# Score products of prompt attention in pairs of units, their low parts on half the array each

## The reference

```python
z = jnp.einsum('bqhd,bkhd->bhqk', q, k) * (HEAD_DIM ** -0.5)
z = z + sb_bias[None, :, None, None]
mask = kpos[None, :] < qpos[:, None]
l = jnp.where(mask, jax.nn.log_sigmoid(-z), 0.0)
later = jnp.flip(jnp.cumsum(jnp.flip(l, -1), -1), -1) - l
w = jnp.where(mask, jnp.exp(jax.nn.log_sigmoid(z) + later), 0.0)
out = jnp.einsum('bhqk,bkhd->bqhd', w, v)
```

## Time and profile before

| | |
|---|---|
| median of three timed runs | 2445.37 us (2442.97 to 2445.67) |
| span of the profiled execution | 2440.8 us (its own total time is not on the page) |
| busy: PE, its weight loads, DVE, ACT | 99%, 96%, 65%, 53% |
| score products on the low part of the keys | 160, from 410 to 1578 us |

### The profile page before, as it was taken

One profiled execution on the slowest core, in us unless ns is written; L12 is line 12 of the kernel. 1 busy time (PEld: TensorE's weight loads), 2 busy tenths in 40 slices (PEclk: granted clock), 3 DMA queues, 4 the chain that ended last, 5 costly groups with the idle time before them and its releaser, 6 DMA issues.

```text
span 2440.8 us, 36724 instructions
## 1 busy us (share of the span) xinstructions
PE 2406.7 (99%) x13263; PEld 2331.5 (96%) x13263; DVE 1585.0 (65%) x2233; ACT 1286.6 (53%) x1982; POOL 243.0 (10%) x527
## 2 busy tenths in 40 slices
PE   7999999999999999999999999999999999999998
PEld 7999999999999999999999999999999999999998
DVE  7635662656777787777788777757655665764335
ACT  5466523555655745656555565554455555444432
POOL 0012320200001100011100111000122130000000
PEclk9999999999999999999999999999999999999999
DMA  8434554534444434444443443333566674343332
GB/s 257 153 108 143 159 174 138 184 111 130 162 134 139 142 110 144 150 129 144 128 124 117 137 141 124 125 122 114 182 187 187 209 234 134 120 136 117 112 118 83
DMA packets 141526, 351.64 MB, mean 144 GB/s; under 512 B 20625, under 2 KB 64146, under 8 KB 141218
## 3 DMA queue, kind: packets, MB, share of 16 engines
q1 hardware_dynamic: 128994, 312.88, 40.6%
q0 software_dynamic: 12352, 36.42, 4.7%
HBM read 300.11 MB, written 49.12 MB: 143 GB/s over the span
## 4 chain that ended last, share of the span: by engine, by line
PE 95%; DVE 2%; ACT 2%; DMA 1%; issue 1%; SPq 0%; DVEq 0%; ACTq 0%
PE PS L1136 22%; PE PS L1138 22%; PE PS L1137 22%; PE PS L874 5%; PE PS L872 5%; PE PS L873 5%; PE PS L942 2%; PE PS L964 1%; PE PS L932 1%; PE PS L963 1%; PE PS L1026 1%; PE PS L933 1%; PE PS L1056 1%; PE PS L1014 1%; PE PS L912 1%
## 5 line engine op out<-in xcount | busy, mean ns | idle before, releaser
L1440 ACT ACTIVATE w_hi_lo<-w_raw 128x1024 fp32r<-128x1024 f32 x240 | 252.7, 1053 | 283.5 <-PE PS L1138 277.3
L1136 PE MATMUL PS<-a_hi,w_hi_lo 128*128 128x416 f32 x1080 | 385.1, 357 | 1.3 <-DVE w_hi_lo L1995 1.3
L1138 PE MATMUL PS<-a_hi,w_hi_lo 128*128 128x416 f32 x1080 | 379.3, 351 | 0.0
L1137 PE MATMUL PS<-a_lo,w_hi_lo 128*128 128x416 f32 x1080 | 378.6, 351 | 0.0
L1995 DVE TENSOR_TENSOR w_hi_lo<-w_raw,w_hi_lo 128x1024 fp32r<-128x1024 f32 x240 | 292.6, 1219 | 58.1 <-ACT w_hi_lo L1440 55.9
L1136 PE MATMUL PS<-h_hi,w_hi_lo 128*128 128x416 f32 x824 | 294.6, 358 | 0.0
L1138 PE MATMUL PS<-h_hi,w_hi_lo 128*128 128x416 f32 x824 | 290.2, 352 | 0.0
L1137 PE MATMUL PS<-h_lo,w_hi_lo 128*128 128x416 f32 x824 | 289.4, 351 | 0.0
L2022 DVE TENSOR_TENSOR h_lo<-h_full,h_hi 128x416 fp32r<-128x416 f32 x160 | 94.6, 592 | 222.9 <-ACT h_hi L1455 222.8
L1136 PEld LDWEIGHTS PS<-a_hi,w_hi_lo 128*128 128x128 f32 x1080 | 203.0, 188 | 4.1 <-DVE w_hi_lo L1995 1.7
L1137 PEld LDWEIGHTS PS<-a_lo,w_hi_lo 128*128 128x128 f32 x1080 | 203.5, 188 | 2.1
(11 more groups left out here) (336 smaller groups left out, 5203.8 us busy)
## 6 DMA issues: line engine op xcount, KB each, us to landing
w_raw<-w_all SPq DMA_DIRECT2D x380, 512.0 KB, 3.5
proj_scratch<-stage SPq DMA_DIRECT2D x70, 208.0 KB, 1.9
k_rows<-kv_out SPq DMA_DIRECT2D x80, 128.0 KB, 4.0
v_hi_lo<-v_scratch SPq DMA_DIRECT2D x40, 256.0 KB, 4.1
x_scratch<-x_full SPq DMA_DIRECT2D x20, 416.0 KB, 2.9
x_residual<-x_scratch SPq DMA_DIRECT2D x5, 1664.0 KB, 7.6
pages<-ck SPq DMA_DIRECT2D x64, 128.0 KB, 2.2
pages<-ck POOLq DMA_DIRECT2D x64, 128.0 KB, 2.5
```

Of the source, the lines that this page charges most:

```text
L1136: pe.matmul(out, w_h, mh_[:, k, :], start=(g == 0), stop=False)
L1137: pe.matmul(out, w_h, ml_[:, k, :], start=False, stop=False)
L1138: ins = pe.matmul(out, w_l, mh_[:, k, :], start=False, stop=(g == KT - 1))
L1440: act.activation(halves(w_hi(n)), raw_halves(n), ACT.Copy).then_inc(s_wh, 1)
```

## The change

Units are scored in pairs in the even slots. The two products with the keys' high part stay as they are. The product with the low part now takes the high part of q alone: 64 rows, rows 0 to 63 for the even unit and 64 to 127 for the odd one. For that, DVE puts the low part of q into the lower rows of odd units and the upper rows of even units (the product of the two low parts is left out). Even units use bank 6, odd ones bank 4. Bank 4 is thus no longer free for the value tiles: they are turned in bank 3, between the last sum of one head and the first of the next. Such a turn waits for the head before (`HEADS_BEFORE`), and the first sum of a head waits for the tiles turned so far. Steps and slots of the turns are moved accordingly.

```diff
-V_AT_STEP = {78: 0, 81: 1, 83: 2}
-V_AT_SLOT = {24: 3, 40: 4, 60: 5, 80: 6, 110: 7}
+V_AT_STEP = {78: 0, 82: 1, 84: 2}
+V_AT_SLOT = {28: 3, 44: 4, 64: 5, 88: 6, 116: 7}
+HEADS_BEFORE = (0, 1, 2, 5, 7, 9, 11, 13)
...
-    return len(V_AT_STEP) + len([t for t in V_AT_SLOT if t < tau])
+    return len([j for j in V_AT_STEP if 2 * (j - 78) < tau]) + len([t for t in V_AT_SLOT if t < tau])
+
+
+def z_bank(t):
+
+    return 4 if t % 2 else 6
...
-            def scores(t):
-
-                v, i, w, top = unit(t)
+            def scores_two(t):
+
+                v, i, _, _ = unit(t)
...
-                q = qs[:, (c * NH + h) % 2, i * P:(i + 1) * P]
-                pe.matmul(PS[:, 6, 0:w], q, khl[:, v % 2, 0, 0:w], start=True, stop=False)
-                pe.matmul(PS[:, 6, 0:w], q, khl[:, v % 2, 1, 0:w], start=False, stop=True).then_inc(s_z, 1)
+                for d in range(2):
+                    w = unit(t + d)[2]
+                    q = qs[:, (c * NH + h) % 2, (i + d) * P:(i + d + 1) * P]
+                    pe.matmul(PS[:, z_bank(t + d), 0:w], q, khl[:, v % 2, 0, 0:w], start=True, stop=False)
+                for d in range(2):
+                    w = unit(t + d)[2]
+                    high = slice(HD * d, HD * d + HD)
+                    q = qs[high, (c * NH + h) % 2, (i + d) * P:(i + d + 1) * P]
+                    pe.matmul(PS[:, z_bank(t + d), 0:w], q, khl[high, v % 2, 1, 0:w], start=False, stop=True).then_inc(s_z, 1)
...
                 if m:
-                    pe.wait_ge(s_vlo, m)
+                    pe.wait_ge(s_yc, HEADS_BEFORE[m])
                 for j in range(4):
-                    ins = pe.transpose(PS[:, 4, j * P:(j + 1) * P], vmk[:, 0, j, :].bitcast(F32), ident[:, :])
+                    ins = pe.transpose(PS[:, 3, j * P:(j + 1) * P], vmk[:, 0, j, :].bitcast(F32), ident[:, :])
...
+                if v in FIRST:
+                    pe.wait_ge(s_vlo, v_tiles_done(4 * v + 6))
...
-                if tau < N_UNITS:
-                    scores(tau)
+                if tau < N_UNITS and tau % 2 == 0:
+                    scores_two(tau)
...
-                dve.tensor_tensor(qs[HD:P, w % 2, :], qst[HD:P, :], qs[HD:P, w % 2, :].bitcast(F32), ALU.subtract).then_inc(s_qlo, 1)
+                full = qst[:, :].rearrange("p (i two q) -> p two i q", two=2, q=P)
+                parts_ = qs[:, w % 2, :].rearrange("p (i two q) -> p two i q", two=2, q=P)
+                for odd, low in ((0, slice(HD, P)), (1, slice(0, HD))):
+                    ins = dve.tensor_tensor(parts_[low, odd], full[low, odd], parts_[low, odd].bitcast(F32), ALU.subtract)
+                ins.then_inc(s_qlo, 1)
```

More of the change, by code:

```diff
@@ L1383, in round_v @@
                 act.wait_ge(s_vtr, m + 1)
-                act.activation(vmk[:, :, :, 0:HD], PS[:, 4, :].rearrange("p (j h d) -> p h j d", h=2, d=HD), ACT.Copy).then_inc(s_vhi, 1)
+                act.activation(vmk[:, :, :, 0:HD], PS[:, 3, :].rearrange("p (j h d) -> p h j d", h=2, d=HD), ACT.Copy).then_inc(s_vhi, 1)
             def sigmoids(t):
@@ L1394, in sigmoids @@
                     act.wait_ge(s_tr, t - 2)
-                act.activation(sP[:, t % 3, 0:w], PS[:, 6, 0:w], ACT.Sigmoid, scale=HD ** -0.5, bias=bias_h[:, h:h + 1])
+                act.activation(sP[:, t % 3, 0:w], PS[:, z_bank(t), 0:w], ACT.Sigmoid, scale=HD ** -0.5, bias=bias_h[:, h:h + 1])
                 if t >= 5:
@@ L1398, in sigmoids @@
                     act.wait_ge(s_car, t)
-                act.activation(nP[:, t % 5, 0:w], PS[:, 6, 0:w], ACT.Sigmoid, scale=-HD ** -0.5, bias=nbias_h[:, h:h + 1]).then_inc(s_sn, 1)
+                act.activation(nP[:, t % 5, 0:w], PS[:, z_bank(t), 0:w], ACT.Sigmoid, scale=-HD ** -0.5, bias=nbias_h[:, h:h + 1]).then_inc(s_sn, 1)
             def round_w(t):
@@ L1939, in round_v @@
                 dve.wait_ge(s_vhi, m + 1)
-                dve.tensor_tensor(vmk[:, :, :, HD:P], PS[:, 4, :].rearrange("p (j h d) -> p h j d", h=2, d=HD),
+                dve.tensor_tensor(vmk[:, :, :, HD:P], PS[:, 3, :].rearrange("p (j h d) -> p h j d", h=2, d=HD),
                                   vmk[:, :, :, 0:HD].bitcast(F32), ALU.subtract).then_inc(s_vlo, 1)
```

## The result

The changed kernel takes 2455.18 us (median of four runs, 2454.19 to 2455.59), the kernel before 2444.17 (four runs, 2441.43 to 2445.67): 1.0046 of it, with an interval of 1.0033 to 1.006. It is slower by 11.0 us. The forecast was slower by 22.4: the direction and the place are right, and the size is twice what was measured. The time lies in the forecast's range, but only because that was taken down through the unchanged case; it is under the likeliest case's own range (2457 to 2477). All times here are of runs at a granted clock of 0.996 to 0.998; one run among the experiments, at 0.557, took 4016 us and is left out.

What follows compares the result with a forecast made beforehand. The prediction took the matrix engine, busy 99% of the span, as the bound. Low products in pairs +24.4 us and the wait that goes -2 gave +22.4; 2445.4 + 22.4 = 2468 us, slower by 0.9%, range 2441 to 2480.

Steps and rivals of the forecast that it cites:

- the unchanged case: Low products do not overlap and no way in and out is paid: 2443 us, no change; chance 0.09, with mixed cases.
- the likeliest case: Low products pay for a change of mode, 80 times: slower, own range 2457 to 2477 us, chance 0.74.
- What bounds the kernel: Whole span: matrix engine busy 99%, 95% of the last chain; only its work or gaps gain or lose time.
- The way in: Before a pair's first low product: 0.09 us of emptying, then 0.11 for a 128-column load, 0.20 in all.
- Between the two low products: Within a pair's low part: the second product starts 0.11 us after the first, and they overlap from there.
- rival 2: The mode changes, but a pair's low products start together: +15.6 - 2, 2459 us; counted in the 0.74 for slower.
- The way out: Behind a pair's low products: 0.08 us of emptying and 0.11 until the next product streams, 0.19 in all.
- The wait that goes: Three odd units' score products no longer wait for the sigmoid emptying bank 6: between nothing and 2.7 us, taken as -2.
- Value tiles and the q split: Value tiles turned in bank 3, and the vector engine's q subtraction split into two halves: cost 0 each.
- 1 (no mode, 2430): 64 rows are no other mode and the low products run together: 15.8 us faster, 2430; chance 0.17.
- 3 (no overlap, 2474): Low products do not overlap at all; with the way in and out +31 - 2, 2474 us; counted in the 0.74.

## Why the forecast had the direction and missed the size

**What bounds the kernel**: right. The loss is on the matrix engine, and the slots of attention account for all of it, as the sum below shows.

**The way in**: right, 0.21 (0.10 + 0.11) for the forecast 0.20. What stood only on eight products of 32 rows and 32 columns holds for 64 rows and 128 columns. The price is paid at each change of height: the 80 more ways in and out of the run with each unit alone cost 0.37 us each. The Trainium skill, "TensorEngine Tiling (Array Packing)", section "Key Properties", has the rule that a change of mode drains the engine; these traces agree with it for 64 rows. A change of columns alone, from 128 to 32, shows no gap.

**Between the two low products**: the step that failed. The forecast took 0.11 for the second load, from two loads that follow each other on the same rows. On separate rows the loads run together, 0.19 for both, and so do the products; on the same rows the loads take 0.29. That term is 80 x 0.11 = 8.8 us too large. The alternative stood in the text as rival 2. The Trainium skill, "TensorE: Matmul & The Clock Gate", section "Measured speedup vs the span model", gives about 4 ns for each further tile. This case's trace agrees: 3 or 4 ns between the starts of the two products.

**The way out**: mis-sized, 0.14 (0.08 + 0.06) for 0.19. The forecast used the load of a dense product, from the way out of the 32-row products; here transposes follow, whose load is recorded with 0.14 in place of 0.19 (a single one, in the changed kernel):

```profile
648.69 0.14 PEld L954 LDWEIGHTS PS<-ident,s_prompt 128*128 128x128 f32 x1 [0.24 <-issue]
```

The run with the low products first shows the 0.05. Times 80 pairs that is 4.0 us too large.

**The sum again**, from rows: +24.4 - 8.8 - 4.0 = +11.6; the 0.01 more of the way in adds 0.8, and the -2 of the wait is left out, for the reason below. For all three kinds of pairs the changed kernel can also be set against the one with full rows, start of the first score product to the second product behind the transposes. At (512, 512) that is +0.12. For (384, 512) and (128, 256), first the changed kernel:

```profile
647.76 0.57 PE L940 MATMUL PS<-k_hi_lo,q_hi_lo 128*128 128x384 f32 x2
...
649.09 0.40 PE L978 MATMUL PS<-wT_lo,v_hi_lo 128*128 128x512 f32 x1
...
683.10 0.39 PE L940 MATMUL PS<-k_hi_lo,q_hi_lo 128*128 128x128 f32 x2
...
684.42 0.35 PE L1151 MATMUL PS<-h_lo,w_hi_lo 128*128 128x416 f32 x1
```

and the one with full rows:

```profile
645.29 0.56 PE L940 MATMUL PS<-k_hi_lo,q_hi_lo 128*128 128x384 f32 x2
...
646.46 0.39 PE L977 MATMUL PS<-wT_lo,v_hi_lo 128*128 128x512 f32 x1
...
680.26 0.39 PE L940 MATMUL PS<-k_hi_lo,q_hi_lo 128*128 128x128 f32 x2
...
681.36 0.35 PE L1150 MATMUL PS<-h_lo,w_hi_lo 128*128 128x416 f32 x1
```

+0.16 (1.33 against 1.17) and +0.22 (1.32 against 1.10). 48 x 0.12 + 16 x 0.16 + 16 x 0.22 = 11.8 us, against 11.0 measured (8 to 15 by the interval). These are single pairs; the medians over all pairs of a kind differ by 0.11, 0.17 and 0.23, which makes 11.7.

**The wait that goes**: a second, smaller step that failed. It went at all three places, but the 2 us did not come with it. On the product side, before and after (total us, times, longest):

```profile
PE PS L932 <- ACT n_prompt L1399: 1.7, 3, 0.7
PE PS L954 <- DVE s_prompt L1976: 1.7, 2, 1.4
```

The products waited 1.7 us for the sigmoids and now wait 1.7 us for the vector engine, which the forecast did not reckon with; its 2.7 was the loads' idle, of which the products feel a part. At the 70th unit the engine waits all the same, now in front of the transposes:

```profile
853.59 0.66 PE L954 MATMUL PS<-ident,s_prompt 128*128 128x128 f32 x4 [1.36 <-DVE s_prompt L1976]
```

Before, once the sigmoid had let the score products of that unit go, the transposes' load stood 0.35 us for the vector engine's product all the same:

```profile
847.55 0.42 PEld L942 LDWEIGHTS PS<-ident,s_prompt 128*128 128x128 f32 x4 [0.35 <-DVE s_prompt L1958]
```

The score products ran in the shadow of that wait, and taken out of the slot they only lengthen it: from the last dense product ahead to the second one behind it is 2.39 us in both kernels. At the other two places 0.5 us each went from the products, and 0.3 came back in a second wait for the vector engine; in the run with full rows what is left can't be told from zero.

**Value tiles and the q split**: right, no cost. Neither the turns' wait for the head before nor the weighing's for a tile's low part is listed; the one wait of a turn is for its DMA, 0.6 us of the loads, 0.7 before. The tile turned behind head 6 (slot 44) follows that slot's transposes without a wait:

```profile
706.92 0.55 PE L954 MATMUL PS<-ident,s_prompt 128*128 128x128 f32 x3
707.31 0.60 PE L963 MATMUL PS<-ident,v_made 128*128 128x128 f32 x4
```

**The rivals**: 1 (no mode, 2430) is out; 3 (no overlap, 2474) is what the run on the same rows shows, 2469; 2 (start together, 2459) came nearest. Without its -2 and with the way out at its real price it gives +11.6, against 11.0 measured; its time is off by a little more, as the kernel before took 2444.2 in these runs and not the 2445.4 that it starts from.

## What to carry to other kernels

Two half-height products side by side save one product but pay a way in and a way out: here 0.23 us saved against 0.35 paid per pair. Such a block pays only if it holds enough products for the saving to pass the price of its two changes; with pairs it doesn't, and with the mode changed for each unit it is far worse. By these numbers two pairs in one block would just pay, 0.46 saved against 0.35; that is an estimate, and no run here tried it. And a price taken from the nearest row should be taken apart first, into emptying, load and product, and each part set for the operands that will really stand there: the neighbour's load and the row group decided half of this sum.

## What the runs showed of the hardware

Two weight loads on separate halves of the array take the time of one (0.19 us recorded for both, 0.29 on the same half), and the two products run together. A change between 128 and 64 rows leaves 0.08 to 0.10 us of emptying and then the part of the next load that is no longer hidden: 0.06 of a transpose's, 0.11 of a product's. And the first product behind such a change has a longer record, whatever its height: with each unit by itself, 0.49 us for 64 and for 128 rows at 512 columns, against 0.40 for the product ahead of the change. Its record starts with its load (668.54 for both). So behind a change of height the starts of the records have to be read together with the loads.
